# Six more gate/up pairs computed with seven products, some of them next to each other

## What is computed

```python
def _swiglu(x, w_gu, w_down):
    g, u = jnp.split(x @ w_gu, 2, axis=-1)
    return (jax.nn.silu(g) * u) @ w_down
...
    mod = (silu_c @ w_mod[l] + b_mod[l]).reshape(B, N_MOD, D_MODEL)
    h = h + 0.5 * m[2][:, None] * _swiglu(_modulate(_rms(h, norm_w[l, 0]), m[0], m[1]),
                                          ffn1_w_gu[l], ffn1_w_down[l])
```

## Time and profile before

| | |
|---|---|
| runs | 1619.53 us median of 3 (1618.72 to 1620.03) |
| profiled execution | 1620.21 us, span 1618.5 us |
| TensorE, VectorE, ScalarE, GpSimd busy | 99%, 77%, 43%, 5% |
| seven-product pairs in stages 0, 1, 2 | 4, 9, 9 |
| read from memory | 247.88 MB, 154 GB/s over the span |

### The profile page before, as it was taken

One profiled execution on the slowest core, in us unless ns is written; L12 is line 12 of the kernel. 1 busy time (PEld: TensorE's weight loads), 2 busy tenths in 40 slices (PEclk: granted clock), 3 DMA queues, 4 the chain that ended last, 5 costly groups with the idle time before them and its releaser, 6 DMA issues.

```text
span 1618.5 us, 24338 instructions
## 1 busy us (share of the span) xinstructions
PE 1608.7 (99%) x9468; PEld 1405.3 (87%) x9468; DVE 1246.1 (77%) x1908; ACT 693.6 (43%) x1062; POOL 84.7 (5%) x149
## 2 busy tenths in 40 slices
PE   8999999999999999999999999999999999999999
PEld 4888888889878898999988898999988997999888
DVE  5887777897878678788878788888766587887654
ACT  5422233324856454333343154333433274665542
POOL 0000000110000100000000000001000000100000
PEclk9999999999999999999999999999999999999999
DMA  9455555653321223344445433446645332365554
GB/s 376 155 189 175 170 171 166 187 207 104 104 79 50 81 92 110 138 169 156 162 143 190 169 106 131 143 158 207 209 156 204 123 117 81 114 197 183 184 190 147
DMA packets 69614, 250.47 MB, mean 155 GB/s; under 512 B 7552, under 2 KB 8576, under 8 KB 69376
## 3 DMA queue, kind: packets, MB, share of 16 engines
q1 hardware_dynamic: 51072, 181.84, 34.1%
q0 software_dynamic: 18432, 67.12, 12.0%
HBM read 247.88 MB, written 1.05 MB: 154 GB/s over the span
## 4 chain that ended last, share of the span: by engine, by line
PE 95%; DVE 3%; ACT 1%; DMA 0%; issue 0%; DVEq 0%; ACTq 0%
PE ps L1702 28%; PE ps L1703 28%; PE ps L1704 28%; PE ps L1745 3%; PE ps L1793 2%; PE ps L1746 2%; PE ps L1795 1%; PE ps L2111 1%; PE ps L1854 1%; PE ps L2079 1%; PE ps L2093 0%; DVE nmax L1509 0%; DVE shared_b L1180 0%; DVE wlo L989 0%; PE ps L1824 0%
## 5 line engine op out<-in xcount | busy, mean ns | idle before, releaser
L989 DVE TENSOR_TENSOR wlo<-raw,whi 128x1024 fp32r<-128x1024 f32 x320 | 387.4, 1223 | 212.1 <-ACT whi L551 209.8
L1702 PE MATMUL ps<-xh,whi 128*128 128x512 f32 (+1 forms) x1404 | 489.5, 349 | 2.6 <-DVE xl L1188 2.3
L551 ACT ACTIVATE whi<-raw 128x1024 fp32r<-128x1024 f32 x320 | 335.3, 1055 | 346.7 <-PE ps L1704 261.8
L1703 PE MATMUL ps<-xl,whi 128*128 128x512 f32 (+1 forms) x1404 | 481.7, 343 | 0.0
L1704 PE MATMUL ps<-xh,wlo 128*128 128x512 f32 (+1 forms) x1404 | 481.3, 343 | 0.0
L1702 PEld LDWEIGHTS ps<-xh,whi 128*128 128x128 f32 x1404 | 266.0, 189 | 39.7 <-DVE xl L1188 4.5
L1703 PEld LDWEIGHTS ps<-xl,whi 128*128 128x128 f32 x1404 | 266.1, 190 | 30.9 <-issue 0.7
L1704 PEld LDWEIGHTS ps<-xh,wlo 128*128 128x128 f32 x1404 | 265.9, 189 | 31.2
L1703 PE MATMUL ps<-al,whi 128*128 128x512 f32 (+2 forms) x768 | 263.4, 343 | 0.0
L1702 PE MATMUL ps<-ah,whi 128*128 128x512 f32 (+1 forms) x668 | 235.6, 353 | 0.0
L1704 PE MATMUL ps<-ah,wlo 128*128 128x512 f32 (+1 forms) x668 | 235.0, 352 | 0.0
(11 more groups left out here) (218 smaller groups left out, 2368.6 us busy)
## 6 DMA issues: line engine op xcount, KB each, us to landing
raw<-wstream SPq DMA_DIRECT2D x320, 512.0 KB, 3.5
wm<-wmod POOLq DMA_DIRECT2D x128, 512.0 KB, 4.7
wm<-wmod SPq DMA_DIRECT2D x8, 1024.0 KB, 16.6
h<-x_t SPq DMA_DIRECT2D x4, 512.0 KB, 6.1
cb<-cols SPq DMA_DIRECT2D x1, 1024.0 KB, 20.2
out_t<-h SPq DMA_DIRECT2D x8, 128.0 KB, 2.7
K<-cols SPq DMA_DIRECT2D x1, 907.0 KB, 20.6
K<-cols SPq DMA_DIRECT2D x1, 265.5 KB, 2.8
```

What stands on the lines that cost most here:

```text
L551: act.activation(whi[:, n % SPL, :, :].rearrange("p a b -> p (a b)"), raw[:, n % RING, :], ACT.Copy)\
L989: dve.tensor_tensor(wlo[:, n % RING, :, :].rearrange("p a b -> p (a b)"), raw[:, n % RING, :], whi[:, n % SPL, :, :].rearrange("p a b -> p ...
L1702: pe.matmul(out_ap, hi_w, hi_x, start=start, stop=False)
L1703: pe.matmul(out_ap, hi_w, lo_x, start=False, stop=False)
```

## The change

The tables now name 28 pairs, (6, 11, 11) by stage, and in stages 1 and 2 four couples of neighbours: 4 and 5, 7 and 8, 10 and 11, 13 and 14. For the second of each couple (`SECOND`) there is a second place for the weight sums, and its banks are 7 and the two that the plain pair would have. Every seven-product pair now uses three banks only: the first product goes to the right half of the bank that the fourth and sixth use too, so ScalarE copies it out ahead of everything else in the iteration (`first_copy`), and TensorE waits for that copy before the fourth product. The first copy has two buffers; the sums of the gate's first half now lie in `ups`, so the last addition waits for the first silu (`silu_a`). The modulation pairs are dealt out anew with the same totals; those in the down loop stay.

```diff
-SEVENS = ((7, 11, 15, 19),
-          (4, 6, 8, 10, 12, 14, 16, 18, 20),
-          (4, 6, 8, 10, 12, 14, 16, 18, 20))
-MODS_GU = ({2: 1, 3: 1, 4: 2, 5: 2, 7: 2, 8: 2, 9: 2, 11: 2, 12: 2, 13: 2, 15: 2, 16: 2, 17: 2, 19: 2, 20: 2, 21: 1},
-           {1: 1, 5: 1, 7: 2, 9: 2, 10: 1, 11: 1, 12: 1, 13: 1, 14: 1, 15: 2, 17: 2, 19: 2, 20: 1},
-           {1: 1, 5: 1, 6: 1, 7: 2, 9: 2, 11: 2, 12: 1, 13: 2, 14: 2, 15: 2, 16: 2, 17: 2, 18: 2, 19: 2, 20: 2})
+SEVENS = ((7, 9, 11, 14, 17, 19),
+          (4, 5, 7, 8, 10, 11, 13, 14, 16, 18, 20),
+          (4, 5, 7, 8, 10, 11, 13, 14, 16, 18, 20))
+MODS_GU = ({2: 1, 3: 1, 4: 2, 5: 2, 6: 2, 8: 2, 9: 1, 10: 2, 11: 1, 12: 2, 13: 2, 14: 1, 15: 2, 16: 2, 18: 2, 19: 2, 20: 2},
+           {1: 1, 2: 1, 6: 2, 9: 2, 12: 2, 14: 1, 15: 2, 16: 1, 17: 2, 19: 2, 20: 2},
+           {1: 1, 2: 1, 6: 2, 9: 2, 11: 2, 12: 2, 13: 2, 14: 2, 15: 2, 16: 2, 17: 2, 18: 2, 19: 2, 20: 2})
...
+SECOND = ((), (5, 8, 11, 14), (5, 8, 11, 14))
...
+        s32s, shis, slos = (s32, s32_more), (shi, shi_more), (slo, slo_more)
...
+        def seven_banks(f, j):
+            return (7, 2 * j % 4, 2 * j % 4 + 1) if sums_at(f, j) else (4, 5, 6)
...
+            def first_copy(f, j):
+
+                k = seventh(f, j)
+                if k >= 2:
+                    act.wait_ge(two_done, k - 1)
+                act.wait_ge(product1, k + 1)
+                act.activation(firsts[:, k % 2, :], ps[:, seven_banks(f, j)[2], S:T], ACT.Copy).then_inc(s1_done, 1)
+
             def silu_seven(f, j):
 
                 k = seventh(f, j)
-                act.wait_ge(product1, k + 1)
                 act.wait_ge(mul_done, FC * f + j - 1)
-                act.activation(ups[:, 0:S], ps[:, 7, 0:S], ACT.Copy).then_inc(s1_done, 1)
...
                 for j in range(FC):
                     n = n0 + 2 * j
+                    if seven(f, j):
+                        first_copy(f, j)
                     if not seven(f, j + 2) and not seven(f, j + 1):
                         split_next(n)
...
-                    if seven(f, j + 1):
+                    if seven(f, j + 1) and not seven(f, j + 2):
                         split_next(n)
                     if not seven(f, j + 2):
                         split_next(n + 1)
...
-                if k:
-                    dve.wait_ge(products43, k)
-                h = KQ * P
+                if sums_used(f, j):
+                    dve.wait_ge(product3, sums_used(f, j))
+                h, s32 = KQ * P, s32s[sums_at(f, j)]
...
                 dve.wait_ge(s1_done, k + 1)
-                dve.wait_ge(products26, k + 1)
-                dve.tensor_tensor(pair_of(first_up), twice(ups[:, 0:S]), pair_of(ps[:, 4, :]), ALU.add)\
+                dve.wait_ge(product6, k + 1)
+                dve.wait_ge(mul_done, FC * f + j)
+                dve.tensor_tensor(pair_of(ups), twice(firsts[:, k % 2, :]), pair_of(ps[:, first, :]), ALU.add)\
                     .then_inc(gate_a, 1)
...
+                dve.wait_ge(silu_a, k + 1)
                 dve.tensor_tensor(ups.rearrange("p (s h t) -> p h s t", s=2, h=2),
...
                 pe.wait_ge(lo_done, n + 1)
-                product(7, 0, in_block(gate, 0), half(0, 0)).then_inc(product1, 1)
-                product(4, 0, in_block(gate, KQ), half(KQ, 0)).then_inc(block_done, 1)
+                product(two, S, in_block(gate, 0), half(0, 0)).then_inc(product1, 1)
+                product(one, 0, in_block(gate, KQ), half(KQ, 0)).then_inc(block_done, 1)
                 pe.wait_ge(lo_done, n + 2)
                 pe.wait_ge(tlo_done, 4 * f + 4)
-                product(5, 0, in_block(up, KQ), of_x(3))
-                product(6, 0, in_block(up, 0), of_x(1)).then_inc(block_done, 1)
+                product(four, 0, in_block(up, KQ), of_x(3))
+                pe.wait_ge(s1_done, k + 1)
+                product(two, 0, in_block(up, 0), of_x(1)).then_inc(block_done, 1)
                 pe.wait_ge(slo_done, k + 1)
-                product(4, S, of_sums(1), of_x(2)).then_inc(products26, 1)
-                product(6, S, of_sums(0), of_x(0)).then_inc(products75, 1)
-                product(5, S, of_sums(2), half(KQ, 1)).then_inc(products43, 1)
+                product(one, S, of_sums(1), of_x(2)).then_inc(product6, 1)
+                product(two, S, of_sums(0), of_x(0)).then_inc(product5, 1)
+                product(four, S, of_sums(2), half(KQ, 1)).then_inc(product3, 1)
```

More of the change, by code:

```diff
@@ L189, in program @@
         sums.close()
+        more = ExitStack()
+        more.enter_context(nc.sbuf_tensor("more_behind", [P, 16 * T], F32))
+        s32_more = more.enter_context(nc.sbuf_tensor("s32_more", [P, 3, KQ * P], F32))
+        shi_more = more.enter_context(nc.sbuf_tensor("shi_more", [P, 3, KQ, P], F32R))
+        more.close()
+        more_low = ExitStack()
+        more_low.enter_context(nc.sbuf_tensor("more_low_behind", [P, 16 * T], F32))
+        slo_more = more_low.enter_context(nc.sbuf_tensor("slo_more", [P, 3, KQ, P], F32R))
+        more_low.close()
+        s32s, shis, slos = (s32, s32_more), (shi, shi_more), (slo, slo_more)
         x32 = hid[:, 11 * T:19 * T].rearrange("p (c s h t) -> p c s h t", c=DC, s=2, h=2)
@@ L340, in program @@
         product1 = sem("product1")
[L341 to L343 removed]
+        product6 = sem("product6")
+        product5 = sem("product5")
+        product3 = sem("product3")
         s1_done = sem("s1_done")
         gate_a = sem("gate_a")
+        silu_a = sem("silu_a")
         two_done = sem("two_done")
@@ L442, in seventh, with sums_at, sums_used @@
             return sum(len(SEVENS[i]) for i in range(f)) + SEVENS[f].index(j)
+        def sums_at(f, j):
+            return int(j in SECOND[f])
+        def seven_banks(f, j):
+            return (7, 2 * j % 4, 2 * j % 4 + 1) if sums_at(f, j) else (4, 5, 6)
+        def sums_used(f, j):
+            same = [seventh(g, i) for g in range(DEPTH + 1) for i in SEVENS[g]
+                    if (g, i) < (f, j) and sums_at(g, i) == sums_at(f, j)]
+            return max(same) + 1 if same else 0
         def sevens_until(f):
@@ L1085, in weight_sums_low @@
                 dve.wait_ge(shi_done, seventh(f, j) + 1)
-                dve.tensor_tensor(slo[:, :, :, :].rearrange("p k c n -> p (k c n)"),
-                                  s32[:, :, :].rearrange("p k n -> p (k n)"),
-                                  shi[:, :, :, :].rearrange("p k c n -> p (k c n)").bitcast(F32), ALU.subtract)\
+                a = sums_at(f, j)
+                dve.tensor_tensor(slos[a][:, :, :, :].rearrange("p k c n -> p (k c n)"),
+                                  s32s[a][:, :, :].rearrange("p k n -> p (k n)"),
+                                  shis[a][:, :, :, :].rearrange("p k c n -> p (k c n)").bitcast(F32), ALU.subtract)\
                     .then_inc(slo_done, 1)
@@ L1101, in seven_begin @@
                 k = seventh(f, j)
+                first, _, two = seven_banks(f, j)
                 dve.wait_ge(s1_done, k + 1)
-                dve.wait_ge(products26, k + 1)
-                dve.tensor_tensor(pair_of(first_up), twice(ups[:, 0:S]), pair_of(ps[:, 4, :]), ALU.add)\
+                dve.wait_ge(product6, k + 1)
+                dve.wait_ge(mul_done, FC * f + j)
+                dve.tensor_tensor(pair_of(ups), twice(firsts[:, k % 2, :]), pair_of(ps[:, first, :]), ALU.add)\
                     .then_inc(gate_a, 1)
                 dve.wait_ge(gate_a, k + 1)
-                dve.wait_ge(products75, k + 1)
-                dve.tensor_tensor(pair_of(two_ups), twice(first_up[:, S:T]), pair_of(ps[:, 6, :]), ALU.add)\
+                dve.wait_ge(product5, k + 1)
+                dve.tensor_tensor(pair_of(two_ups), twice(ups[:, S:T]), pair_of(ps[:, two, :]), ALU.add)\
                     .then_inc(two_done, 1)
@@ L1914, in of_sums @@
                 def of_sums(i):
-                    return lambda q: (shi[:, i, q, :], slo[:, i, q, :])
+                    return lambda q: (shis[a][:, i, q, :], slos[a][:, i, q, :])
                 def half(c, h):
```

25 lines of the change are left out of this document (15 added, 10 removed).

## The result

The changed kernel takes 1630.94 us (median of 4 runs, 1628.39 to 1633.85), the kernel before 1619.45 beside it (1618.72 to 1620.03): a ratio of 1.0069, 95% interval [1.0057, 1.0082]. It is slower, by 11.5 us where +6.4 was forecast, and 1630.94 lies 0.44 us above the upper end of the range.

A forecast was written before the change was run, and what follows sets the result against it. TensorE was taken as the bound, its saved columns and new waits counting in full: -4.98 + 1.98 + 2.52 + 0.2 + 0.5 + 6.2 = +6.4 us, 1625.9 us in terms of medians, range 1619.5 to 1630.5.

The forecast's parts named there:

- The gain of 4.98: On TensorE: six more seven-product pairs, each 10.08 us instead of 10.91, save 6 x 0.83 = 4.98 us.
- Pair 14 of f2: Before product four there, TensorE waits 6.2 us for ScalarE's late first copy.
- the chain: VectorE's steps in f2 from pair 8's last addition, modulation included: copy of pair 14 ends at 62.1, due 56.11.
- The rival of no stall in pair 14: In f2, silu of 13 goes before the modulation, so 6.2 us falls away: 1619.7, chance 0.10.
- The clock: TensorE's clock behind the 6.2 us gap in pair 14 of f2: no loss taken, bounds nothing to 5.8 us.
- the prediction's rival for pair 14: TensorE's clock falls in that gap of f2, sum some 2 to 3 us higher: 1628.8, chance 0.30.
- The wait on tlo in f1: Pair 4, before product three: the modulation pair added in j = 2 makes tlo late, a stall of 1.98 us.
- In f2, where 2.52 was forecast: Pair 4, before product three: tlo already at the limit, so the added modulation pair's 2.52 us come through in full.
- The thin margins and pair 5: Second neighbours in f1 and f2 wait for the copy: 0.5 us for pairs 8, 11, 14; 0.2 for pair 5.
- The margin of 0.08: Second neighbours in f1 and f2: the first copy is ready 0.08 us before it would stall product four.
- the rival of 2.5 us from it: Five second pairs each stall 0.6 us if the chain misses 0.5: +2.5, 1628.4, chance 0.10.
- The rival that ended faster: VectorE always arrives in time in f1 and f2, TensorE waits for nothing: 1614.6, chance 0.08.

The follow-up runs named there:

- both_moved: Changed kernel with the edits of x_moved and m14_moved together: 1615.13 us, 0.9967 of the kernel before.
- m13_moved: x_moved, and of f2 only the two modulation pairs of j = 13 moved, to j = 21 and the down loop: 1616.21 us, 0.998 of the kernel before.
- x_moved_copy_early: x_moved, and ScalarE makes the second neighbour's first copy between the two silus of the first: 1621.43 us, 1.0008 of the kernel before.
- m14_moved: Changed kernel with f2's modulation pairs of j = 11 and 13 thinned out to j = 8, 21 and the down loop: 1621.03 us, 1.0007.
- filled: Changed kernel with matmuls whose output nobody reads in TensorE's three gaps, all waits kept: 1626.86 us, 1.0038 of the kernel before.
- before_mod2: Kernel before with only its modulation pair of j = 5 moved to j = 2 in f1 and f2: 1625.95 us, 1.0036 of the kernel before.
- x_moved: Changed kernel with only its modulation pair of j = 2 moved to j = 5 in f1 and f2: 1623.27 us, 1.0018 of the kernel before.

## Why the prediction was right or wrong

**The gain of 4.98: right.** Undisturbed, pairs 5, 7 and 8 of f1 in after take 10.08 us (643.67 to 653.75, 664.66 to 674.73 to 684.81), and both_moved gains 5.1.

**Pair 14 of f2: right, and nearer than the chain deserves.** The chain has the last addition of pair 13 at 59.0 after that of pair 10 (21.69): 37.3 us. VectorE's timeline in after, its ends and the places between, and ScalarE's:

```profile
1066.07 0.42 DVE L1155 TENSOR_TENSOR shared_b<-shared_b,ps 128x256 f32<-128x256 f32 x1
...
1084.80 1.22 DVE L1041 SCALAR_TENSOR_TENSOR shared_a<-wm,cb 128x1024 f32<-128x1024 f32 x1
1089.84 0.69 DVE L1055 TENSOR_TENSOR hid<-shared_b,ps 128x512 f32<-128x512 f32 x1
...
1097.04 1.22 DVE L1041 SCALAR_TENSOR_TENSOR shared_a<-wm,cb 128x1024 f32<-128x1024 f32 x1
1102.18 0.69 DVE L1141 TENSOR_TENSOR shared_a<-shared_b,ps 128x512 f32<-128x512 f32 x1 [0.25 <-DVE wm L1041]
1103.62 0.42 DVE L1155 TENSOR_TENSOR shared_b<-shared_b,ps 128x256 f32<-128x256 f32 x1
...
1102.96 0.42 ACT L630 ACTIVATE shared_b<-shared_a 128x256 f32<-128x256 f32 x1 [8.38 <-DVE shared_a L1141]
1104.08 0.42 ACT L633 ACTIVATE shared_b<-shared_b 128x256 f32<-128x256 f32 x1 [0.70 <-DVE shared_b L1155]
1104.40 1.99 ACT L575 ACTIVATE whi<-raw 128x1024 fp32r<-128x1024 f32 x2
1106.30 0.36 ACT L622 ACTIVATE shared_b<-ps 128x256 f32<-128x256 f32 x1
```

It is 1103.62 - 1066.07 = 37.55. Two modulation pairs stand between 1084.80 and the product at 1089.84, and two more between 1097.04 and the addition at 1102.18; then silu, two splits, copy, in this order, the copy ending 3.0 behind the addition (3.06 forecast). The stall is 6.25 for 6.2. That it agrees to 0.05 is luck: VectorE was 0.24 later than the chain has it, and product four started 0.05 us behind the end of the copy's row (1106.66) and not 0.21. Take the two modulation pairs of j = 13 out of the chain and it stays right (m13_moved); take the splits out and TensorE waits that much less (x_moved_copy_early); take one of j = 11 out as well and the stall is gone (m14_moved). The rival of no stall in pair 14 fell with the first trace. (The last addition of pair 11 is 1.2 late by the chain's own figures and not 1.3; nothing hangs on it.)

**The clock: wrong, and the largest miss.** The failed step is the term for TensorE's clock, "I take nothing, the nearest row's value". The row was of the end of the kernel, where nothing follows that could have been seen to run slowly. In after the clock fell at all three gaps and cost 6.1 us in the profiled execution and 4.1 to 4.9 in the medians (filled). The rival had the mechanism and a chance of 0.30, but for one gap alone; the other two I had myself forecast at 2.0 and 2.5 us, and never asked of them. By the rule of the Trainium skill, "TensorE: Matmul & The Clock Gate", Part 1, an array left idle goes to 1.2 GHz and comes back after sustained work. The trace of after agrees in that: behind the gap of f1 the granted clock is 0.52 of 2.4 GHz from 634, and 1.00 again from 640. The 2 to 3 us of the prediction's rival for pair 14 were 1.9.

The end was not the longest idle of TensorE in the trace of before either. At the start it waits 3.76 us for constants, and the first five matmuls behind that wait go at half the pace of the later ones of the same shape: 5 in 4.53 us, a little later 11 in 4.88. Timeline and windows of before:

```profile
3.76 4.53 PE L1854 MATMUL ps<-K 128*128 128x512 f32 x5 [3.76 <-DMA K<-cols]
...
8.56 4.88 PE L1854 MATMUL ps<-K 128*128 128x512 f32 x11
...
4.00:8.00 4.00, 4.00 (x5) 1.61 (x6) 1.50 (x4) 3.07 (x5) 0.00 (x0) 1.00 0.90 320
9.00:13.00 4.00, 4.00 (x11) 1.85 (x10) 3.53 (x6) 3.37 (x5) 0.00 (x0) 1.00 1.04 421
```

The column of the granted clock says 1.00 in both windows, and only the number of matmuls shows the difference. This does not show a fall, as nothing runs ahead of it, but it is a row of the low pace behind an idle time of under 4 us, and it would have spoken for the rival.

**The wait on tlo in f1: right in kind, too small.** 1.98 was forecast and 3.13 measured. The sum took the places of before as they were and put 2.52 us on top. But the due time moved too. The last of ScalarE's splits that VectorE waits for at the start of the stage waits itself for its block from memory; rows of before and then of after:

```profile
604.26 1.06 ACT L551 ACTIVATE whi<-raw 128x1024 fp32r<-128x1024 f32 x1 [0.18 <-DMA raw<-wstream]
```

```profile
603.24 1.06 ACT L575 ACTIVATE whi<-raw 128x1024 fp32r<-128x1024 f32 x1 [1.15 <-DMA raw<-wstream]
...
612.89 0.69 DVE L1055 TENSOR_TENSOR hid<-shared_b,ps 128x512 f32<-128x512 f32 x1 [0.50 <-DVE wm L1041]
...
629.01 4.62 DVE L1098 TENSOR_TENSOR tlo<-t,thi 128x1024 fp32r<-128x1024 f32 x4
```

It starts 28.27 ahead of product three's due time in before (632.53), 27.41 in after (630.65). That is 0.86 of the 1.15 missing. The idle time of VectorE ahead of `hid` at 612.89, behind the modulation pair of j = 1, is some 0.3 longer than in before; both_moved has the same 0.50 there, so the moved pair doesn't make it, and what does is not known. The block's landing differs by execution: the same place had 2.15 in m14_moved, 1.84 in before_mod2, 2.60 in filled. In f2, where 2.52 was forecast, it was 3.06 in after, 1.91 in m14_moved, 2.98 in before_mod2 and 1.9 in filled. So one value from one trace stood for something that varies by over 1 us; a range of 1.8 to 3.1 for each place would have been honest. That this pair causes both waits is shown by x_moved and before_mod2.

**The thin margins and pair 5: 0.7 forecast, nothing measured.** The view of waits has one wait on the copy, pair 14's. The second neighbours 5, 8 and 11 have no gap, nor does any pair of f0. The margin of 0.08 held, and the rival of 2.5 us from it fell. Pair 5 could not be judged in after, where the slow clock gave the copy of pair 5 time; in filled, without it, pair 5 takes 10.16 us in f1, 0.1 late as forecast, and 10.08 in f2; in m14_moved, with the clock at 1.00 in f1 as well, it takes 10.07.

**The sum again**, in the profiled execution: waits 12.4 where 11.4 stood, clock 6.1 where 0 stood; 1620.21 - 4.98 + 12.4 + 6.1 = 1633.8, and 1633.85 was measured. In the medians, +11.5 for +6.4, the clock's 4.1 to 4.9 us are nearly all of the difference. The rival that ended faster, "at most 0.8 us late there, and tlo before product three", named the two conditions correctly: both_moved meets them, and its 1614.6 came out as 1615.1. They were not met by the change itself.

## What to carry to other kernels

Where TensorE is the bound, price a new wait twice: the gap, and what its clock costs behind it, here 1.4 to 2.7 us each time it fell. In this kernel it fell behind most gaps from 1.9 us upward, though not behind every one. Saved products come in full only if the in-order queues of the other engines are followed through the whole run of dense pairs: a movable work item of 2.5 us is free in one iteration and on the critical path in the next, and two neighbours in a table decide it. Price against the median, not against the one execution that was profiled: here the two lay up to 2.9 us apart. Look for a clock fall by the number of matmuls in a window, since the busy share stays at 100%, and where a gap can't be removed, matmuls into a free bank keep the clock, but too many of them make the wait longer (0.7 us in pair 4 of f2 in filled).

## What the runs showed of the hardware

- The length of a gap did not decide by itself whether the clock fell. It fell at gaps of 1.91 (m14_moved, f2), 2.98, 3.06, 3.13, 3.78, 6.25 and 6.3 us; it stayed at 1.00 after 1.09, 1.84 and 2.15 (m14_moved, f1, the same execution as the 1.91).
- At the low level a matmul of 256 columns starts some 0.21 us after the last, at the high one 0.120.
- A longer gap did not cost more clock: 1.9 us behind the 6.25 of pair 14, 2.7 behind the 3.13 of f1. Only that part of a low stretch costs anything in which TensorE has work. In pair 14 the clock was low already in the last 2.7 us of the gap, and then for 4.1 us of work; in f1 for 0.8 us of the gap and 5.9 of work; in f2 it fell when work had begun again, for 3.3. The losses of 1.88, 2.69 and 1.56 us are each a little under half of that work. Windows of after:

```profile
633.00:639.70 6.70, 5.92 (x28) 5.95 (x29) 6.63 (x9) 2.54 (x2) 0.00 (x0) 0.50 0.10 40
994.80:998.10 3.30, 3.30 (x18) 3.30 (x17) 3.23 (x5) 1.94 (x2) 0.00 (x0) 0.50 0.00 0
1104.00:1106.70 2.70, 0.00 (x0) 0.00 (x0) 2.56 (x5) 2.58 (x4) 0.00 (x0) 0.50 0.62 193
1106.70:1110.80 4.10, 4.09 (x19) 4.09 (x20) 3.52 (x6) 0.00 (x0) 0.53 (x1) 0.50 0.07 10
```

- How long it stays low differs from place to place, and from run to run: the four runs of after have spans of 1632.2, 1630.3, 1628.2 and 1626.7 us at mean granted clocks of 0.995, 0.996, 0.997 and 0.997, and with the gaps filled the clock is 1.00 each time and the spread 1.8 us, not 5.5. Which of the gaps differ between those runs isn't known, since only one of them has a trace.
